# A hybrid decoder layer's mixture-of-experts step on one core: fixed expert order, three weight sets, and four smaller edits

## The chip, the core and the metric

The kernel runs on one NeuronCore of one Trainium2 chip. Its engines are TensorE (PE, matrix products into the PSUM banks), VectorE (DVE), ScalarE (ACT), GpSimd (POOL, which also issues the indirect transfers) and SyncE (SP, which issues nearly all others). The metric is the device time of one execution in microseconds, as the median of several runs.

## The reference

One layer over 1104 tokens: 64 tokens of 8 short sample sequences with states of their own, 16 meta tokens and 1024 prompt tokens. The mixer projects each token, applies a causal convolution, runs a gated delta rule (GDN, 4 heads) and a Mamba-2 recurrence (SSD, 8 heads), and projects back; the residual and a layer norm follow. Then comes a mixture of experts over the 1088 tokens that are kept (no meta tokens), two experts a token:

```python
def _moe(h, router_g, router_e, w1, w3, w2):
    g_val, g_idx = lax.top_k(g_prob, 1)
    ...
    e_val, e_idx = lax.top_k(jax.nn.softmax(e_logits, axis=-1), TOP_K)
    gate = g_val * e_val / jnp.sum(e_val, axis=-1, keepdims=True)
    expert = g_idx * E_PER_GROUP + e_idx
    ...
        xb = h[tok]
        return (jax.nn.silu(xb @ w1[e]) * (xb @ w3[e])) @ w2[e]
```

and y is the gate-weighted sum over a token's experts. D_MODEL is 1024, an expert is 512 wide, there are 32 experts. A last residual and layer norm give the output. Everything is float32.

## The kernel before, in words

The program is a chain of stages with a barrier between them. Each stage writes every engine's instructions by hand, so an engine's order is the order of its code, and semaphores (wait_ge, then_inc) join the engines.

**Projection and mixer.** After the projections, a mixer stage walks nine tiles: tile 0 holds the 64 sample tokens and the 16 meta tokens, tiles 1 to 8 hold 128 prompt tokens each. While tile 0 is worked, PE fills its waits with pieces of a gate projection (gate_part(n), L763). For tile 0 the state of every sample sequence has to be read: sample_ssd multiplies 32 state tiles (4 chunks ch[c] by 8 sequences, the state being the stationary operand) with 8 columns each (L974), ScalarE copies the result to rh, and 4 transposes (L979) turn it round. sample_gdn does the same with 16 columns (L1002), copies to rs, and adds rs with products against the identity (L1011, L1017). Both rs and rh hang on a memset (m_rs) for which PE waits at the start of the stage.

In the prompt loop, i is the tile in preparation, p = i-1 the one being finished, r = i-2 the one whose layer-normed row x1 goes through x1_transpose (L931), x1_copy (L1253) and router (L938). out_project (L962) is the projection back. In the last two rounds nothing is prepared, and PE does x1_transpose and router of tile 7 ahead of mix_transpose (L945, L948) and out_project of tile 8.

**Router stage.** DVE works out top-1 group, top-2 experts, the counts per expert, and a slot for each of the 2176 token-expert pairs in blocks of 96 (BLK). An expert has at least one block. Blocks lie in the order of the experts; table[0] is the last block's number and table[1 + n] block n's expert. SP loads expert 0's weights meanwhile (6 transfers of 1 MB: w13 in quarters q, w2 in halves).

**Expert stage.** A loop with a run-time end over the blocks. For block b PE does h_transpose(b-1) (L2116), x_transpose(b+1) (L2099), up(b) (L2109: 96 products, three thirds r, each ending in an e_up) and down(b-1) (L2130: 48 products in three thirds, each ending in an e_out). There is one set of w13 buffers and one of w2, so SP loads a quarter of the next block as soon as a third of up(b) has read its own (L2034), and w2 likewise after thirds of down (L2037); the very last block's w2 has buffers of its own (w2e). POOL gathers the block's 96 token rows into the one buffer xg (L2071) and adds the outputs to d_acc in HBM (L2077) from the one buffer eo. DVE's take(n) writes the row numbers to gather when block n-1 has been transposed, gate does the products with SiLU, and mark(n) the row numbers to add to, when the addition before has landed. ScalarE's evict(n) waits for both mark(n) and that addition.

**Final stage.** Nine tiles of d_acc are read back. DVE does the statistics of a tile (L2273, L2277, L2279), POOL the power -1/2 (L2315), DVE the shift (L2284), ScalarE the scaling (L2308), DVE the gain (L2289), POOL the offset (L2320) for seven tiles and DVE (L2292) for the last two; SP stores.

The input has 33 blocks: 33 additions to d_acc are in the trace, so one expert has two blocks and 31 have one.

## Time and profile before

| | |
|---|---|
| median of 3 runs | 1706.05 us (1699.59 to 1706.51) |
| the profiled execution: its own time, its span | 1698.48 us, 1696.6 us |
| busy share of the span: PE, DVE, ACT, POOL | 87%, 32%, 25%, 18% |
| mean granted TensorE clock | 0.938 of full |
| HBM read, written | 284.08 MB, 48.14 MB |
| mean DMA rate over the span | 193 GB/s |
| stages by their start in the trace | mixer 351 us, router 969 us, experts 1005 us, final 1650 us |

The times below are microseconds from the start of the span. The busy shares are means over stages that have different limits, so each stage has to be read by itself. The profiled execution lies at the fast end of the runs.

### The profile page before, as it was taken

How to read it: one execution, taken by the hardware profiler on the slowest of the kernel's cores; microseconds unless marked ns; L12 is line 12 of the kernel's file. 1: busy time of each engine (PE TensorE's matmuls, PEld its weight loads, DVE VectorE, ACT ScalarE, POOL GpSimd, SP SyncE). 2: the span in 40 equal slices, each digit the busy share in tenths (PEclk: the TensorE clock that was granted, in tenths of full speed). 3: DMA queues.
4: the chain of work that ended last, by engine and by line, in shares of the span. 5: the costliest groups of instructions: out<-in, count | busy, mean ns of one | idle time of the engine just before them, and what ended most of it. 6: DMA issues, size and time to landing. Idle time of an engine off the chain costs nothing. (4 is left out here: it accounts for less than half of the span.)

```text
span 1696.6 us, 34800 instructions
## 1 busy us (share of the span) xinstructions
PE 1477.5 (87%) x14148; PEld 977.6 (58%) x14148; DVE 545.9 (32%) x1257; ACT 427.8 (25%) x1207; POOL 297.2 (18%) x247
## 2 busy tenths in 40 slices
PE   8999999979898999999997528999999999899950
PEld 5666666657556777777775324555555555555530
DVE  2444444322134554445552251111111111111108
ACT  2211111131034344444342001222222222222212
POOL 0000000020114434224431000111111111111116
PEclk9999999998899999999999658999999999999985
DMA  7233332151325212222201246999999999999944
GB/s 255 78 91 80 78 79 69 51 173 40 113 77 209 87 44 75 100 100 82 97 29 38 91 184 221 375 379 383 376 366 378 377 373 378 383 369 373 384 114 190
DMA packets 119239, 328.24 MB, mean 193 GB/s; under 512 B 42712, under 2 KB 72328, under 8 KB 92552
## 3 DMA queue, kind: packets, MB, share of 16 engines
q1 hardware_dynamic: 110296, 300.59, 48.0%
q0 software_dynamic: 7728, 22.29, 5.6%
q10 hardware_dynamic: 1152, 4.52, 0.7%
q8 instruction: 39, 0.64, 0.2%
q14 instruction: 24, 0.20, 0.0%
HBM read 284.08 MB, written 48.14 MB: 196 GB/s over the span
## 5 line engine op out<-in xcount | busy, mean ns | idle before, releaser
L2109 PE MATMUL bank<-sb_arena 128*32 128x256 f32 x6336 | 352.2, 382 | 36.2 <-DMA sb_arena<-w 35.1
L387 PE MATMUL bank<-sb_arena 128*128 128x368 f32 x1056 | 329.8, 475 | 6.3 <-DMA sb_arena<-xT 6.3
L2109 PEld LDWEIGHTS bank<-sb_arena 128*32 128x32 f32 x6336 | 202.9, 111 | 175.8 <-DMA sb_arena<-w 40.8
L387 PEld LDWEIGHTS bank<-sb_arena 128*128 128x128 f32 x1056 | 201.3, 191 | 132.7 <-DMA sb_arena<-w_conv 6.3
L2130 PE MATMUL bank<-sb_arena 128*32 128x256 f32 x3168 | 177.8, 380 | 11.3 <-issue 6.7
L2130 PEld LDWEIGHTS bank<-sb_arena 128*32 128x32 f32 x3168 | 102.8, 110 | 83.8 <-issue 18.0
L962 PE MATMUL bank<-sb_arena 128*128 128x512 f32 (+1 forms) x288 | 133.9, 606 | 6.3 <-DVE sb_rlog L1566 5.0
L2216 DVE SCALAR_TENSOR_TENSOR sb_arena<-sb_arena,bank 128x128 f32<-128x128 f32 x99 | 28.6, 289 | 340.2 <-ACT sb_arena L2168 340.2
L2077 POOL DMA_INDIRECT d_acc<-sb_arena,sb_oidx x33 | 47.6, 1443 | 511.3 <-ACT sb_arena L2182 511.3
L2168 ACT ACTIVATE sb_arena<-bank 128x128 f32<-128x128 f32 x99 | 27.4, 277 | 373.8 <-PE bank L2109 373.8
L763 PE MATMUL bank<-sb_arena 128*128 128x384 f32 (+1 forms) x288 | 99.6, 499 | 8.5 <-DVE sb_arena L1582 8.5
L1516 DVE TENSOR_TENSOR sb_arena<-sb_arena,bank 128x256 f32<-128x256 f32 (+1 forms) x102 | 41.2, 412 | 153.8 <-PE bank L882 100.2
L962 PEld LDWEIGHTS bank<-sb_arena 128*128 128x128 f32 (+1 forms) x288 | 50.9, 188 | 60.6 <-issue 58.8
L763 PEld LDWEIGHTS bank<-sb_arena 128*128 128x128 f32 x288 | 55.9, 201 | 44.3 <-DVE sb_arena L1582 9.1
L459 DVE SCALAR_TENSOR_TENSOR sb_arena<-sb_arena 128x1040 f32<-128x1040 f32 x60 | 78.1, 1302 | 2.1
L1730 POOL TENSOR_TENSOR sb_arena<-sb_arena,sb_mask 128x512 f32<-128x512 f32 x48 | 72.6, 1519 | 13.2 <-DVE sb_arena L1425 4.9
L1763 POOL TENSOR_TENSOR sb_arena<-sb_arena 128x512 f32<-128x512 f32 (+1 forms) x9 | 11.0, 1220 | 363.8 <-ACT sb_arena L1158 363.8
L862 PE MATMUL bank<-sb_arena 128*128 128x128 f32 (+1 forms) x408 | 58.5, 290 | 14.8 <-DVE sb_arena L1516 14.2
L2208 DVE TENSOR_SCALAR sb_idx<-sb_slot 96x1 int32 (+1 forms) x35 | 5.2, 148 | 199.5 <-PE bank L2099 199.5
L862 PEld LDWEIGHTS bank<-sb_arena 128*128 128x128 f32 (+1 forms) x408 | 54.6, 202 | 25.5 <-issue 23.6
L1220 ACT ACTIVATE sb_arena<-bank 128x256 f32<-128x256 f32 (+1 forms) x102 | 38.6, 378 | 117.6 <-PE bank L862 114.8
L2181 ACT ACTIVATE sb_arena<-bank 96x256 f32<-96x256 f32 x99 | 37.5, 379 | 101.8 <-PE bank L2130 95.7
(325 smaller groups left out, 1710.8 us busy)
## 6 DMA issues: line engine op xcount, KB each, us to landing
sb_arena<-w SPq DMA_DIRECT2D x198, 1024.0 KB, 9.5
sb_arena<-w_conv SPq DMA_DIRECT2D x28, 512.0 KB, 4.8
sb_arena<-d_conv SPq DMA_DIRECT2D x7, 1792.0 KB, 7.1
d_conv<-sb_arena SPq DMA_DIRECT2D x22, 512.0 KB, 3.2
sb_arena<-d_gam SPq DMA_DIRECT2D x8, 768.0 KB, 3.9
d_x<-sb_arena SPq DMA_DIRECT2D x9, 512.0 KB, 2.7
sb_arena<-xT ACTq DMA_DIRECT2D x8, 552.0 KB, 9.2
sb_arena<-w_out SPq DMA_DIRECT2D x8, 512.0 KB, 7.1
```

Of the source, the lines that this page charges most:

```text
L387: last = e.matmul(bank[3 * r + s][:, 0:TN], wring[n % NV][:, k, :], xT[:, k, TN * s:TN * s + TN], start=(k == 0), stop=(k == KT - 1))
L459: e.scalar_tensor_tensor(aP, raw[r][:, i:i + TP], convw[:, n, i:i + 1], aP, ALU.mult, ALU.add)
L763: mm = e.matmul((D0, D1)[j % 2][:, 0:c1 - c0], gw[m % NSLOT][:, k, :], xT[:, k, c0:c1], start=(k == 0), stop=(k == KT - 1))
L862: last = e.matmul(bY[0:n, q * P:q * P + n], bt[level % 2][0:n, h0 + q, 0:n], X[0:n, h0 + q, 0:n], start=True, stop=True)
L962: last = e.matmul((D0, D1)[half][0:m, :], mixT[:, k, 0:m], wo[:, k, half * 512:(half + 1) * 512], start=(k == 0), stop=(k == KT - 1))
L1220: e.activation(ys[0:n, h0:h0 + 2, 0:n], heads(bY)[0:n, 0:2, 0:n], ACT.Copy).then_inc(S[f"lv_ys{s}"], 1)
L1516: e.tensor_tensor(d, d, heads(bZ)[0:n, 0:2, 0:n], ALU.subtract).then_inc(S[f"lv_x{s}"], 1)
L1730: e.tensor_tensor(bt[level % 2][0:n, :, 0:n], at[0:n, :, 0:n], bc1(mk(i)[0:n, LV + level, 0:n], n, GH, n), ALU.mult).then_inc(S["lv_bt"], 1)
L2077: e.indirect_dma_start(a["d_acc"], bass.IndirectOffsetOnAxis(ap=oidx[:, 0:1], axis=0), eo[0:BLK], None, compute_op=ALU.add).then_inc(S["e_ ...
L2109: mm = e.matmul(bank[r][j * CG:(j + 1) * CG, 0:2 * P], xgT[:, k, g * CG:(g + 1) * CG], w13[quarter_of(j, r)][:, k, :], start=(k == 0), sto ...
L2130: mm = e.matmul(bank[6 + r % 2][j * CG:(j + 1) * CG, 0:256], h, w[c // 2][:, k, (c % 2) * 256:(c % 2 + 1) * 256], start=(k == 0), stop=(k ...
L2181: e.activation(eo[0:BLK, r * 256:(r + 1) * 256], out[0:BLK, 0:256], ACT.Copy)
```

## The change

Five edits come together.

1. **Expert order and weights.** Blocks are worked in a new order: first the first block of each expert 0 to 31, then the blocks left over. order[n] is the place of the n-th worked block in the slot table; DVE reads it with a register load (place) ahead of take, gate and mark. There are three whole sets of weight buffers (NSET), with semaphores W of their own. Experts 0, 1 and 2 are loaded in the router stage, 18 transfers. In the expert stage SP's program is written out for experts 3 to 31, with fixed addresses, each quarter waiting for the third of up three blocks before; blocks left over are loaded into set 1 (LATER) alone, each after the block ahead of it. w2e is gone. PE's loop holds three blocks. The last block's outputs go to a buffer eo_last with row numbers oidx_last.
2. **Sample tokens of the mixer.** The 8 columns of each sequence are laid into zeroed tiles per_seq of 8 x 64 columns, which are now the stationary operand, and the states are the moving one, summed over the sequences in PSUM. rs, rh, their copies, the transposes and the products with the identity are gone.
3. **End of the prompt loop.** x1_transpose and router of tile 7 come after out_project of tile 8; DVE and ScalarE are reordered to match.
4. **Router stage.** The comparison that finds each block's expert has 22 columns in place of 54; five small instructions fill order.
5. **Final stage.** The gain and offset rows are copied into PSUM first and read from there in halves; the shift is another form of instruction; the statistics of tiles 1, 4 and 7 are done on ScalarE.

The core of the diff:

```diff
+                    gate_part(8)
+                    e.wait_ge(S["m_c"], 2)
...
-                            last = e.matmul(G1[:, c * TS + b * SL:c * TS + b * SL + SL], ch[c][:, b, :], cv[0][:, 18 + c // 2, b * SL:b * SL + SL], start=True, stop=True)
-                    last.then_inc(S["rh_ps"], 1)
-                    gate_part(8)
-                    e.wait_ge(S["rh"], 1)
-                    for c in range(4):
-                        last = e.transpose(G0[0:TS, c * P:(c + 1) * P], rh[:, c, :], ident[:])
+                            last = e.matmul(G0[0:TS, c * P:(c + 1) * P], per_seq[c // 2][:, b * TS:(b + 1) * TS], ch[c][:, b, :], start=(b == 0), stop=(b == SB - 1))
...
-                        e.wait_ge(S[f"ch_in{c}"], 32)
-                        for b in range(SB):
-                            last = e.matmul(G0.rearrange("p (h t s) -> p h t s", h=GH, t=2)[:, c, :, b * SL:b * SL + SL], ch[c][:, b, :],
-                                            qw[:, :, c, b * SL:b * SL + SL], start=True, stop=True)
-                    last.then_inc(S["rs_ps"], 1)
...
+                        e.wait_ge(S["m_w"], h + 1)
+                        e.wait_ge(S[f"ch_in{h}"], 32)
+                        e.matmul(G1[TS:T0, h * P:(h + 1) * P], XT[0:T0, h, TS:T0], vt[0][0:T0, h, :], start=True, stop=True)
+                        e.matmul(G1[0:TS, h * P:(h + 1) * P], XT[0:T0, h, 0:TS], vt[0][0:T0, h, :], start=True, stop=False)
+                        for b in range(SB):
+                            last = e.matmul(G1[0:TS, h * P:(h + 1) * P], per_seq[h % 2][:, b * TS:(b + 1) * TS], ch[h][:, b, :], start=False, stop=(b == SB - 1))
+                        if h < GH - 1:
+                            last.then_inc(S["w_ps"], 1)
+                            e.wait_ge(S["m_q"], h + 1)
+                        else:
+                            last.then_inc(S["u_ps"], 1)
+                            e.wait_ge(S["qd"], 1)
+                        for b in range(SB):
+                            last = e.matmul(G0[0:TS, h * P:(h + 1) * P], per_seq[2 + h % 2][:, b * TS:(b + 1) * TS], ch[h][:, b, :], start=(h == 0 and b == 0), stop=False)
+                        last.then_inc(S["r_ps"], 1)
...
-                        if tail:
-                            x1_transpose(r, 0)
-                            x1_transpose(r, 1)
-                            router(r)
                         if post:
                             e.wait_ge(S["st"], p + 1)
                             mix_transpose(p)
                             out_project(p, 0, 16)
+                        x1_transpose(r, 0)
+                        x1_transpose(r, 1)
+                        router(r)
                         continue
...
+                    if post and not prep:
+                        o_scale_a(p)
+                        s_update(p)
+                        o_scale_b(p)
+                        x1_gain(r)
+                        x1_add(r)
+                        mix_o(p)
+                        res_half(p, 0)
+                        continue
+                    if not prep:
+                        x1_gain(r)
+                        x1_add(r)
+                        logits(r - 1)
+                        logits(r)
+                        continue
...
-                    e.dma_start(w13[q].rearrange("p k n -> p (k n)"), a["w13"][0, q]).then_inc(S["r_w"], 16)
-                for h in range(2):
-                    e.dma_start(w2[h].rearrange("p k n -> p (k n)"), a["w2"][0, h]).then_inc(S["r_w"], 16)
+                for s in range(NSET):
+                    for q in (3, 0, 1, 2):
+                        e.dma_start(w13[s][q].rearrange("p k n -> p (k n)"), a["w13"][s, q]).then_inc(W["w13" + "abcd"[q] + str(s)], 16)
...
-                with e.Fori(1, last) as b:
-                    ex = expert(e.snap(b + 1))
-                    now = expert(b)
-                    e.wait_ge(S["e_up"], 3 * b + 1)
-                    load13(0, ex)
-                    e.wait_ge(S["e_up"], 3 * b + 2)
...
+                def first_down(ex):
+                    for h in range(2):
+                        e.wait_ge(S["e_out"], 3 * (ex - NSET + 1) + h)
+                        load2(h, ex % NSET, a["w2"][ex, h])
+
+                for ex in range(NSET, E):
+                    for q in (0, 1, 3, 2):
+                        e.wait_ge(S["e_up"], 3 * (ex - NSET) + min(q, 2) + 1)
+                        load13(q, ex % NSET, a["w13"][ex, q])
+                    if ex > NSET:
+                        first_down(ex - 1)
+                first_down(E - 1)
+                with e.Fori(E, last + 1) as b:
+                    ex = e.value_load(table[0:1, bass.ds(b - (E - 1), 1)], min_val=0, max_val=E - 1)
+                    e.wait_ge(S["e_up"], 3 * b - 2)
+                    load13(0, LATER, a["w13"][bass.ds(ex, 1), 0].rearrange("x p m -> p (x m)"))
...
                     e.wait_ge(S["e_out"], 3 * b)
-                    load2(w2, 0, now, "w2a")
+                    load2(0, LATER, a["w2"][bass.ds(ex, 1), 0].rearrange("x p m -> p (x m)"))
                     e.wait_ge(S["e_out"], 3 * b + 1)
-                    load2(w2, 1, now, "w2b")
+                    load2(1, LATER, a["w2"][bass.ds(ex, 1), 1].rearrange("x p m -> p (x m)"))
...
-                    scatter(n)
+                    e.wait_ge(S["e_go"], 1)
+                    e.wait_ge(S["e_eo"], n)
+                    e.indirect_dma_start(a["d_acc"], bass.IndirectOffsetOnAxis(ap=oidx_last[:, 0:1], axis=0), eo_last[0:BLK], None, compute_op=ALU.add).then_inc(S["e_st"], 16)
...
+                def up(n, s, load):
+                    e.wait_ge(W[f"w13d{s}"], 16 * load)
                     for r in range(NR):
-                        e.wait_ge(S["w13" + "abc"[r]], 16 * n + 16)
+                        e.wait_ge(W["w13" + "abc"[r] + str(s)], 16 * load)
...
-                with e.Fori(1, last + 1) as b:
+                with e.Fori(0, (E - 2) // NSET) as i:
+                    for j in range(NSET):
+                        before, s = e.snap(NSET * i + j), (j + 1) % NSET
+                        h_transpose(before)
+                        x_transpose(e.snap(NSET * i + (j + 2)))
+                        up(e.snap(NSET * i + (j + 1)), s, e.snap(i + (2 if s == 0 else 1) + (AHEAD if s == LATER else 0)))
+                        down(before, j, e.snap(i + 1 + (AHEAD if j == LATER else 0)))
+                h_transpose(E - 2)
+                x_transpose(E)
+                up(E - 1, LATER, E - 1)
+                down(E - 2, 0, (E - 2) // NSET + 1)
...
-                    down(before, w2)
+                    up(b, LATER, b)
+                    down(before, LATER, before)
                 h_transpose(last)
-                e.wait_ge(S["w2e"], 32)
-                down(last, w2e)
+                down(last, LATER, last)
...
+                e.wait_ge(S["e_og"], last + 1)
+                for r in range(NR):
+                    e.wait_ge(S["e_out"], 3 * last + (r + 2))
...
+                    e.activation(eo_last[0:BLK, r * 256:(r + 1) * 256], out[0:BLK, 0:256], ACT.Copy)
+                    if r == 2:
+                        e.wait_ge(S["e_st"], 16 * last + 16)
...
+                def place(n):
+                    return e.value_load(order[0:1, bass.ds(n, 1)], min_val=0, max_val=NBMAX)
+
                 def take(n, first=False):
+                    at = place(n)
...
                 def mark(n):
+                    at = place(n)
                     e.wait_ge(S["e_st"], 16 * n + 16)
-                    e.tensor_scalar(oidx[:], slot[0:BLK, bass.ds(n, 1)], 1.0, None, ALU.mult).then_inc(S["e_og"], 1)
+                    e.tensor_scalar(oidx[:], slot[0:BLK, bass.ds(at, 1)], 1.0, None, ALU.mult).then_inc(S["e_og"], 1)
...
-                    e.scalar_tensor_tensor(rv[t][0:n, 2:3], mv2[t][0:n, 0:1], -1.0, rv[t][0:n, 1:2], ALU.mult, ALU.mult).then_inc(S["c_nmr"], 1)
+                    if t in BY_ACT:
...
+                        step = e.tensor_scalar(rv[t][0:n, 2:3], mv2[t][0:n, 0:1], rv[t][0:n, 1:2], -1.0, ALU.mult, ALU.mult)
...
-                    e.tensor_tensor(rows[t][0:n], rows[t][0:n], lnrow[0:n, 0, :], ALU.mult).then_inc(S["c_g"], 1)
+                    for s in range(2):
+                        half = rows[t][0:n, s * 512:(s + 1) * 512]
+                        last = e.tensor_tensor(half, half, bank[s][0:n, :], ALU.mult)
...
-                        e.tensor_tensor(rows[t][0:n], rows[t][0:n], lnrow[0:n, 1, :], ALU.add).then_inc(S["c_yv"], 1)
-
-                e.memset(rv[0][0:1, 3:4], 0.0).then_inc(S["c_go"], 1)
+                        for s in range(2):
+                            half = rows[t][0:n, s * 512:(s + 1) * 512]
+                            last = e.tensor_tensor(half, half, bank[2 + s][0:n, :], ALU.add)
+                        last.then_inc(S["c_yv"], 1)
...
+                for q in range(4):
+                    last = e.tensor_copy(bank[q][:], lnrow[:, q // 2, (q % 2) * 512:(q % 2 + 1) * 512])
+                last.then_inc(S["c_ln"], 1)
+                e.wait_ge(S["c_ln"], 1)
...
+                    if t < NTT and t not in BY_ACT:
                         stats(t)
...
-                for t in range(NTT):
...
+                    e.activation(junk[t][0][0:n], rows[t][0:n], ACT.Copy, accum_out=st[t][0:n, 0, 0:1]).then_inc(S["c_sum"], 1)
...
+                    e.activation(junk[t][1][0:n], rows[t][0:n], ACT.Square, bias=st[t][0:n, 0, 1:2], accum_out=st[t][0:n, 0, 2:3]).then_inc(S["c_sq"], 1)
```

The order in which PE's instructions stand, ahead of the loop's end in the expert stage, before. The rows are the body of the loop, one block: h_transpose, x_transpose, up, down, and the branch back.

```order
L2116 MATMUL bank<-sb_ident,sb_arena 128x128 x3
L2095 ISA
L2099 MATMUL bank<-sb_ident,sb_arena 128x96 x8
L2103 ISA
L2109 MATMUL bank<-sb_arena 32x256 x96
L2123 REGISTER_ALU
L2130 MATMUL bank<-sb_arena 32x256 x48
L2137 ISA
L2137 COMPARE_AND_BRANCH
```

The same engine and place in the changed kernel. Two blocks that read like this one stand ahead of it in the same body.

```order
L2170 ISA
L2173 MATMUL bank<-sb_ident,sb_arena 128x128 x3
L2152 ISA
L2156 MATMUL bank<-sb_ident,sb_arena 128x96 x8
L2160 ISA
L2166 MATMUL bank<-sb_arena 32x256 x96
L2182 REGISTER_ALU
L2189 MATMUL bank<-sb_arena 32x256 x48
L2196 REGISTER_ALU
L2196 COMPARE_AND_BRANCH
```

The body has grown from one block to three, and the branch back comes once for three blocks.

The order of PE's instructions in sample_gdn, before: L763 is a piece of the gate projection, L1002 the states against 16 columns, L1010 and L1011 the first head's product and its addition by the identity.

```order
L763 MATMUL bank<-sb_arena 128x384 x8
L1002 MATMUL bank<-sb_arena 128x2x8 x32
L763 MATMUL bank<-sb_arena 128x336 x8
L1010 MATMUL bank<-sb_arena 80x128
L1011 MATMUL bank<-sb_ident,sb_arena 80x128
```

The same place in the changed kernel. L777 is the gate projection; L1022 and L1030 are one head's states as moving operand, 8 sequences each.

```order
L777 MATMUL bank<-sb_arena 128x384 x8
L777 MATMUL bank<-sb_arena 128x336 x8
L1019 MATMUL bank<-sb_arena 16x128
L1020 MATMUL bank<-sb_arena 64x128
L1022 MATMUL bank<-sb_arena 64x128 x8
L1030 MATMUL bank<-sb_arena 64x128 x8
```

The 32 products ahead of the piece of the gate projection have become 16 for each of four heads behind it, and the identity products are gone.

The order of PE's instructions at the end of the prompt loop, before: L853 ends the last state product, L931 and L938 are x1_transpose and router, L945 and L948 mix_transpose, L962 out_project.

```order
L853 MATMUL bank<-sb_arena 128x128 x4
L931 MATMUL bank<-sb_ident,sb_arena 128x128 x8
L938 MATMUL bank<-sb_arena 128x36 x8
L945 MATMUL bank<-sb_ident,sb_arena 128x128 x4
L948 MATMUL bank<-sb_ident,sb_arena 128x128 x4
L962 MATMUL bank<-sb_arena 128x512 x16
L931 MATMUL bank<-sb_ident,sb_arena 128x128 x8
L938 MATMUL bank<-sb_arena 128x36 x8
```

The same place in the changed kernel: L949 and L956 are x1_transpose and router, L963 and L966 mix_transpose, L980 out_project.

```order
L867 MATMUL bank<-sb_arena 128x128 x4
L963 MATMUL bank<-sb_ident,sb_arena 128x128 x4
L966 MATMUL bank<-sb_ident,sb_arena 128x128 x4
L980 MATMUL bank<-sb_arena 128x512 x16
L949 MATMUL bank<-sb_ident,sb_arena 128x128 x8
L956 MATMUL bank<-sb_arena 128x36 x8
L949 MATMUL bank<-sb_ident,sb_arena 128x128 x8
L956 MATMUL bank<-sb_arena 128x36 x8
```

x1_transpose and router of tile 7 have moved from ahead of mix_transpose and out_project of tile 8 to behind them.

## Rows read from the trace of the kernel before

**Rows 1.** Busy time by stretch: length; busy us (instructions) of PE, PEld, DVE, ACT, POOL; clock; DMA share; GB/s.

```profile
969.00:987.00 18.00, 2.29 (x4) 1.17 (x4) 13.53 (x52) 0.44 (x2) 0.00 (x0) 0.50 0.97 395
...
1041.00:1613.00 572.00, 529.66 (x9277) 319.00 (x9277) 70.19 (x281) 135.03 (x372) 73.57 (x61) 1.00 1.01 372
```

**Rows 2.** Waits of PE, 1010 to 1640: total us, times, longest.

```profile
PE bank L2109 <- DMA sb_arena<-w: 35.1, 29, 2.3
```

**Rows 3.** Timeline, 1590 to 1697: start, us, instruction [idle before <- releaser].

```profile
1595.71 10.57 PE L2109 MATMUL bank<-sb_arena 128*32 128x256 f32 x192 [1.11 <-DMA sb_arena<-w]
...
1612.70 10.57 PE L2109 MATMUL bank<-sb_arena 128*32 128x256 f32 x192
...
1636.74 1.93 PE L2130 MATMUL bank<-sb_arena 128*32 128x256 f32 x32 [3.15 <-ACT sb_arena L2182]
```

**Rows 4.** DMA, 1020 to 1600: packets, MB, share; issues, KB, us to landing.

```profile
q0 software_dynamic: 6808, 20.08, 14.5%
q8 instruction: 3, 0.05, 0.0%
...
sb_arena<-w SPq DMA_DIRECT2D x185, 1024.0 KB, 9.5
sb_arena<-d_x,sb_idx POOLq DMA_INDIRECT x32, 10.8
```

**Rows 5.** Timeline, 1000 to 1697: the start of the expert stage.

```profile
1004.71 0.91 DVE L2224 MEMSET sb_arena<- 128x1024 f32 x1 [2.89 <-issue]
...
1007.72 1.18 POOL L2071 DMA_INDIRECT sb_arena<-d_x,sb_idx  x1 [50.00 <-DVE sb_arena L2226]
...
1015.13 1.54 PE L2099 MATMUL bank<-sb_ident,sb_arena 96*128 96x96 f32 x8 [15.35 <-DMA sb_arena<-d_x,sb_idx]
...
1040.85 12.48 PE L2109 MATMUL bank<-sb_arena 128*32 128x256 f32 x192
```

**Rows 6.** Timeline of PE, 378 to 446 (first three) and 440 to 540: sample tokens.

```profile
395.91 10.23 PE L974 MATMUL bank<-sb_arena 128*128 128x8 f32 x64
...
405.99 7.35 PE L763 MATMUL bank<-sb_arena 128*128 128x384 f32 x16
...
414.77 5.43 PE L763 MATMUL bank<-sb_arena 128*128 128x384 f32 x16
...
445.96 3.64 PE L1002 MATMUL bank<-sb_arena 128*128 128x16 f32 x32
...
461.23 6.39 PE L763 MATMUL bank<-sb_arena 128*128 128x336 f32 x16
...
476.38 1.15 PE L1022 MATMUL bank<-sb_arena 16*128 16x128 f32 x8
```

**Rows 7.** Waits of PE, 380 to 470.

```profile
PE bank L1002 <- DMA sb_arena<-state_gdn: 4.6, 2, 2.9
```

**Rows 8.** Timeline, 913 to 1006: the last two tiles of the mixer.

```profile
926.59 1.11 PE L931 MATMUL bank<-sb_ident,sb_arena 128*128 128x128 f32 x4 [5.18 <-DVE sb_arena L1385]
...
933.63 1.09 PE L945 MATMUL bank<-sb_ident,sb_arena 128*128 128x128 f32 x4
...
936.85 16.72 PE L962 MATMUL bank<-sb_arena 128*128 128x512 f32 x32 [1.28 <-DVE sb_arena L1561]
...
953.61 0.69 DVE L1357 SCALAR_TENSOR_TENSOR sb_arena<-sb_arena,bank 128x512 f32<-128x512 f32 x1 [6.07 <-PE bank L962]
...
959.17 0.72 PEld L931 LDWEIGHTS bank<-sb_ident,sb_arena 128*128 128x128 f32 x4 [6.43 <-DVE sb_arena L1385]
```

**Rows 9.** Groups of instructions, 1653 to 1697: busy us, mean ns, idle before.

```profile
L2273 DVE BATCH_NORM_STATS2 sb_arena<-sb_arena 128x6 f32<-128x512 f32 (+1 forms) x18 | 11.5, 676 | 3.5 <-DMA sb_arena<-d_acc 3.5
...
L2315 POOL TENSOR_TENSOR sb_arena<-sb_arena,sb_mhalf 128x1 f32<-128x1 f32 (+1 forms) x9 | 11.0, 1228 | 20.3 <-DVE sb_arena L2279 20.3
```

**Rows 10.** Timeline, 1590 to 1697 and 870 to 1000: single instructions of POOL and DVE.

```profile
1657.13 0.56 POOL L2315 TENSOR_TENSOR sb_arena<-sb_arena,sb_mhalf 128x1 f32<-128x1 f32 x1 [1.11 <-DVE sb_arena L2279]
...
870.50 0.69 DVE L1482 TENSOR_TENSOR sb_arena<-bank,sb_arena 128x512 f32<-128x512 f32 x1 [1.31 <-PE bank L838]
```

245 lines of the change are left out of this document (147 added, 98 removed).

## The prediction

> **What bounds the kernel now.** I read the table of stretches first. In the expert stage, 1041 to 1613, PE is busy 530 of 572 us at the full clock, and the 16 DMA engines are busy throughout at 372 GB/s [rows 1]. So two limits lie close together there, and the other views have to say which one ends last. PE's waits name it: before its first products of a block, PE waits for a weight transfer 29 times, 35.1 us in all [rows 2]. The timeline shows both cases. The up products of one block start at 1595.71 after 1.11 us of such a wait, those of the next at 1612.70 with none, so a block takes PE 16.99 us when its weights are there [rows 3]. From 1040.85 [rows 5] to 1612.70 there are 31 blocks in 571.9 us, 18.45 us each. That is the pace of the transfers: a block's weights are 6.29 MB, its gather and its addition another 20.08 MB / 31 = 0.65 MB [rows 4], and 6.94 MB in 18.45 us is 376 GB/s. The stage is bound by its transfers, with PE 1.46 us a block behind. The router stage is the opposite: in its first 18 us the DMA engines move expert 0's weights at 395 GB/s [rows 1], and then they rest until the expert stage.
>
> **The expert stage, -30 us.** The bytes are the same, 33 x 6.29 MB; 12.6 MB of them move into the time of the router stage. At 395 GB/s that alone is worth 32 us, if no engine becomes the limit before.
> Start: three sets are 18.9 MB, 48 us from 969, landed by 1017; PE's first transposes start at 1015.13 [rows 5]. The first gather, issued at 1007.72, fed them 7.4 us later with the DMA engines free. Now they are loaded, and a gather under load lands after 10.8 us [rows 4], so 3.4 us later. DVE's register load of the place stands ahead of it. The trace has no such load on DVE, but one, of table[0], lies within the 2.89 us of idle ahead of 1004.71 [rows 5], so it costs between 0 and 2.9 us; I take 0, since most of that idle time must be the barrier. In the loop it is hidden: in take and gate DVE waits for PE anyway; in mark it delays oidx, behind which ScalarE's evict and POOL's addition are queued, and PE would wait for evict in the last third of down. Up(1) then starts at about 1044 instead of 1040.85.
> PE's own limit: 30 blocks more at 17.0 us, up(31) at 1554.
> The transfers' limit: the first buffers come free with the first third of up(1), about 1047.5. From there SP is never held up, since PE frees a set every 17.0 us and the DMA engines need 18.45 for one. Expert 4's four quarters take 12.3 us (4/6 of 18.45), each later expert 18.45: those of expert 31 are there at 1047.5 + 12.3 + 27 x 18.45 = 1558, 4 us later than PE wants them. PE begins on three of the four quarters, so up(31) starts at about 1557. The two limits meet at the end of the fixed part: the lead from the router stage is used up just there.
> Last block: the left-over block has one set for itself, set 1, which up(31) is still reading. Its first quarter can be asked for a third, 3.5 us, into up(31), the last two at its end, and ahead of them in SP's queue stand w2 of experts 30 and 31, 12.3 us from 1558 to 1570. Three quarters more take 8.4 us and some 2 us to land: up(32) at 1581, where PE would have been ready at 1574. It ends at 1591.5, and down(31), half as many products, at 1597. w2 of the left-over block is asked for only when down(31) has read the old one, and lands at about 1602; PE wants it at 1599. The last products end at 1608. Before, they end at 1636.74 + 1.93 = 1638.7, and that includes the wait of 3.15 us [rows 3] for the addition ahead of it, which eo_last takes away. Difference -30.
> Bounds: were transfers no limit at all, up(32) would start at 1571 and all end at 1597, -41. Were the rate 365 GB/s (3% less), the same steps give 1626, -12.
>
> **The sample tokens, -8 us.** Before, 64 passes with 8 columns (32 products, two passes each) take 10.1 us, and the gate piece behind them 7.35 us [rows 6]; the next piece of its kind, at 414.77, takes 5.4, so the clock had fallen in between. Now 64 passes with 128 columns and a stationary tile of 64; the gate piece comes first. The nearest row for a pass is L1002 at 445.96, 32 passes in 3.64 us, 0.114 us each [rows 6], so 7.3 us. With 4 transposes gone that is 10.1 + 7.35 + 0.5 against 5.4 + 7.3: -5. In sample_gdn, from 445.96 to 476.38, 30.4 us, 4.6 us are waits for states that are still being loaded [rows 7], and after each of them PE is slower for a time (the gate piece at 461.23 takes 6.39). Now: gate piece 5.4, four heads of 36 passes at 0.114, 16.4; gate piece 5.4; four products 0.9: 28.1, -2, and the third head's state is wanted 8 us later in the sequence than before, so that wait goes. At the start of the stage PE no longer waits for a memset, less than 1. Sum -8. Bounds: a pass may cost 0.157 us as in L974, whose 64 take 10.1: 192 passes more by 0.043, +8, so 0; or the state waits and slow clock go altogether, -11. New waits stand in the heads: on ScalarE's w_columns and on POOL's q_columns, for heads 2 and 3 each behind the head two before; each is one copy of 64 columns and has a head's 4 us to hide in.
>
> **The end of the prompt loop, -6 us.** x1_transpose and router of tile 7 hold PE from 926.59 to 933.63, and out_project of tile 8 starts at 936.85, 3.2 us after mix_transpose begins [rows 8]. With them out of the way mix_transpose waits for the scaling of tile 8's output only. DVE does o_scale before s_update now, so it can start about 925 to 926.5: out_project 7 to 9 us earlier. Behind out_project the 7.0 us of PE's work stand beside the 5.6 us in which DVE works out tile 8's rows (953.61 to 959.17), and tile 8's transposes wait for them (rlog): 1.5 us back. -6, between -4 and -7.5.
>
> **The router stage, 0.** DVE's two comparisons shrink and five small instructions come in, ahead of a wait for PE; PE's work starts no sooner. -1 to +1. SP issues 18 transfers for 6 beside DVE's work, and no longer waits for weights at the end.
>
> **The final stage, -7 us.** POOL's power takes 0.56 us at 1657.13 [rows 10], but 1.23 on average over its nine [rows 9]: an instruction of one column that takes a microsecond is held up. What runs beside the slow ones and not beside the first is DVE's gain, a product of two operands in SBUF. A DVE product with one operand in PSUM takes 0.69 us for half a row at 870.50, beside POOL's work [rows 10]. With the gain read from PSUM nine powers take 5.0 us in place of 11.0, -6, and POOL's power and offset follow each other without a gap before, so all of it shortens the stage; DVE, held up in turn by POOL's offsets, gives 1 to 4 more. The gain itself grows to two instructions of 0.69, and ScalarE's statistics of a tile, which read it twice, delay the scaling of the tile ahead: 1 to 2 back. The four copies into PSUM, 4 x 0.69 = 2.8 us, stand in the 3.5 us in which DVE waits for the first tile [rows 9]; without that cover they would cost all of it. -7. Bounds: POOL stays held up, 0; all holding up goes, -11.
> The Trainium skill (SBUF — State Buffer, Who interferes with whom) has it that VectorE and GpSimd share a pair of ports as an exclusive lock, which a VectorE instruction with two SBUF inputs takes against a GpSimd one that reads SBUF. By that rule all of the holding up goes, the -11 end; the trace agrees as far as 0.56 against 1.23 us shows.
>
> **Sum.** -30 -8 -6 +0 -7 = -51 against the profiled execution's own 1698.5 us: 1647.5. The median of the runs lies 7.6 above that execution and the lowest 1.1; I predict 1649.
>
> **Rivals.**
> PE's code is fetched again at each branch back. In 580 us of the loop PE's instruction queue (q8) moves 3 packets, 0.05 MB [rows 4], so the body of one block stays where it is. The new body is three times as long. If it does not fit, each of 9 branches stops PE for one transfer. No row has the price: a weight transfer lands after 9.5 us under load [rows 4], a free gather after 7.4, and next to nothing is the other end. I take 4: 9 stops make 36 us, of which 11 stand in waits for weights that PE has in the forecast. 25 more: 1674.
> The Trainium skill (Runtime: NRT & Kernel Launch, Instruction fetch mechanics) gives PE a buffer of 128 KiB and says that a branch to code outside the window stops the engine for a fetch. Three blocks are 3 x 598 instructions of 64 bytes, 112 KiB, an estimate from that page that leaves 16 KiB to spare at best, and the page speaks of a smaller window too.
> The same, dearer, is the way to slower: 9 x 7 - 11 = 52, so from 7 us a branch on the whole gain is gone, and at 9.5 us the time is 1647.5 + 74.5 = 1722.
> The transfers run below 372 GB/s with more of them queued: at 365, 18 more, 1665.
> The early loads buy nothing in the expert stage, because gathers behind deeper queues set the pace. A gather has to land inside a block's 17.0 us; it takes 10.8 now. If it takes some 15, the pace is 18.45 again and only the other edits' 21 us are left: 1680. Against it: the loads queued now already keep the engines busy throughout.
>
> **Numbers.** Forecast 0.60, own range 1632 to 1662. Refetching at a middling price 0.17 (1674). Lower rate 0.12 (1665). Gathers 0.06 (1680). Refetching at full price 0.05 (1722). The range 1631 to 1676 takes in the forecast's range, the lower rate and the cheaper half of refetching, 0.8. 0.5% is about what a measurement of this kernel can tell from none, 8.5 us: faster than 1697.5 0.91, within 0.5% 0.05, slower 0.04.
>
> **What would show it.** Right: gaps between the starts of up of 17.0 us, with few waits on weights before block 25; a wait of about 7 us ahead of up(32) and of some 3 ahead of the last down; 395 GB/s from 969 to 1017; the power at 0.56 us in all tiles; out_project of tile 8 within 10 us of the last state product. Wrong: instruction packets by the dozen in the loop with PE idle every third block; gathers landing after 14 us; passes of 0.15 us in the sample products; a stage still at 18.45 a block.

## The result, and the profile after

Slower. The median is 1744.7 us (1740.5 to 1748.3) against 1703.5 for the kernel before beside it, ratio 1.024 (95% interval 1.021 to 1.028). The prediction was 1649 with 1631 to 1676, so it is outside on the slow side, and even beyond what I gave as refetching at full price (1722). The profiled execution has a span of 1746.5 us, 49.9 longer than before.

The page of the changed kernel already has the pattern. Busy tenths of PE in 40 slices of the span, granted clock, DMA, and the instruction queue:

```profile
PE 1497.3 (86%) x14200; PEld 981.6 (56%) x14200; DVE 539.5 (31%) x1269; ACT 435.4 (25%) x1227; POOL 290.8 (17%) x250
...
PE   8999999899989999999986287977977987897970
...
PEclk9999999999989999999997588988988988998985
DMA  7233323152351222211103979989989988988545
...
q8 instruction: 138, 2.26, 0.6%
```

In the right third of the rows, from the start of the expert stage on, most slices have a PEclk of 8 and a dip in PE; a round of three blocks is 1.45 slices long. q8, the instruction queue, has 138 packets. The row on the page of the kernel before has 39, and 3 of them fall in 580 us of its loop [rows 4]:

```profile
q8 instruction: 39, 0.64, 0.2%
```

PE's waits from 950 to 1700 (total us, times, longest), to be read beside [rows 2]:

```profile
PE bank L2173 <- issue: 54.2, 9, 6.6
PE bank L2156 <- issue: 33.7, 9, 4.0
...
PE bank L2189 <- DMA sb_arena<-w: 6.6, 1, 6.6
```

The 29 waits for weights ahead of up are gone; one of 6.6 us is left, ahead of the last products. In their place PE stands idle twice for each of nine branches back, and "issue" says that no data and no semaphore released it. The timeline of PE around one of them:

```profile
1088.79 12.66 PE L2166 MATMUL bank<-sb_arena 128*32 128x256 f32 x192
...
1107.70 10.57 PE L2166 MATMUL bank<-sb_arena 128*32 128x256 f32 x192
...
1124.52 10.57 PE L2166 MATMUL bank<-sb_arena 128*32 128x256 f32 x192
1134.90 5.36 PE L2189 MATMUL bank<-sb_arena 128*32 128x256 f32 x96
1146.22 0.90 PE L2173 MATMUL bank<-sb_ident,sb_arena 128*128 128x128 f32 x3 [5.95 <-issue]
1146.91 1.17 PE L2156 MATMUL bank<-sb_ident,sb_arena 96*128 96x96 f32 x6
1151.93 0.48 PE L2156 MATMUL bank<-sb_ident,sb_arena 96*128 96x96 f32 x2 [3.86 <-issue]
1152.34 13.30 PE L2166 MATMUL bank<-sb_arena 128*32 128x256 f32 x192
```

Between the branches the starts of up are 16.82 us apart, as wanted (1107.70, 1124.52). At the branch PE is idle for 5.95 us at the head of the loop and 3.86 more in the middle of x_transpose, and the up behind it takes 13.30 us in place of 10.57. One round of three blocks takes 1146.22 - 1082.67 = 63.55 us, where 3 x 16.82 are 50.5: 13.1 us a branch, 118 for nine. The clock's share of that, by stretches (length; busy us of PE, PEld, DVE, ACT, POOL; clock; DMA share; GB/s):

```profile
1088.80:1101.40 12.60, 12.60 (x197) 6.66 (x200) 1.59 (x6) 0.56 (x2) 0.98 (x1) 0.83 0.55 175
1107.70:1118.10 10.40, 10.40 (x195) 6.28 (x198) 1.59 (x6) 0.85 (x3) 2.42 (x2) 1.00 1.01 356
1082.70:1146.20 63.50, 53.71 (x897) 31.75 (x897) 7.14 (x27) 13.07 (x36) 7.25 (x6) 0.90 0.92 333
1041.00:1613.00 572.00, 484.09 (x8077) 286.58 (x8073) 64.25 (x243) 117.63 (x324) 65.37 (x54) 0.90 0.92 331
```

In the up behind a stop the granted clock is 0.83 of full on average, in the next one 1.00; against [rows 1] the stage's DMA rate has fallen from 372 to 331 GB/s, because PE frees no buffers while it is idle.

The rest of the program did about what was forecast. The sample tokens, PE's timeline beside [rows 6]:

```profile
391.40 9.89 PE L777 MATMUL bank<-sb_arena 128*128 128x336 f32 x32
401.21 7.20 PE L994 MATMUL bank<-sb_arena 128*64 128x128 f32 x64
...
445.67 1.91 PE L1022 MATMUL bank<-sb_arena 128*64 128x128 f32 x16
447.41 1.91 PE L1030 MATMUL bank<-sb_arena 128*64 128x128 f32 x16
...
468.17 1.15 PE L1040 MATMUL bank<-sb_arena 16*128 16x128 f32 x8
```

The end of the prompt loop, beside [rows 8]:

```profile
914.02 1.06 PE L867 MATMUL bank<-sb_arena 128*128 128x128 f32 x8
...
921.00 16.36 PE L980 MATMUL bank<-sb_arena 128*128 128x512 f32 x32 [1.28 <-DVE sb_arena L1585]
```

The final stage by lines, beside [rows 9] (count | busy us, mean ns | idle before):

```profile
L2437 POOL TENSOR_TENSOR sb_arena<-sb_arena,sb_mhalf 128x1 f32<-128x1 f32 (+1 forms) x9 | 4.9, 548 | 19.9 <-DVE sb_arena L2368 16.9 <-ACT sb_arena L2416 3.0
```

### The profile page after: what moved, and what is told of

The parts are those of the page before. It is cut to its first block and busy times, and to the rows that moved or that the text cites. A ratio compares the mean times of both kernels' runs of the same rounds, so it can differ in the third digit from the quotient of the medians.

```text
span 1746.5 us, 34532 instructions
## 1 busy us (share of the span) xinstructions
PE 1497.3 (86%) x14200; PEld 981.6 (56%) x14200; DVE 539.5 (31%) x1269; ACT 435.4 (25%) x1227; POOL 290.8 (17%) x250
## 5 line engine op out<-in xcount | busy, mean ns | idle before, releaser
L2166 PE MATMUL bank<-sb_arena 128*32 128x256 f32 x6336 | 371.3, 397 | 1.0 <-ACT sb_arena L2227 1.0
L2189 PE MATMUL bank<-sb_arena 128*32 128x256 f32 x3168 | 179.1, 382 | 6.6 <-DMA sb_arena<-w 6.6
L980 PE MATMUL bank<-sb_arena 128*128 128x512 f32 (+1 forms) x288 | 133.6, 604 | 6.3 <-DVE sb_rlog L1590 5.0
L777 PE MATMUL bank<-sb_arena 128*128 128x384 f32 (+1 forms) x288 | 96.1, 486 | 7.7 <-PEq L150 7.7
L2290 DVE TENSOR_SCALAR sb_idx<-sb_slot 96x1 int32 x35 | 5.2, 148 | 266.9 <-PE bank L2156 266.4
L2156 PE MATMUL bank<-sb_ident,sb_arena 96*128 96x96 f32 x272 | 36.9, 284 | 57.5 <-issue 33.7
L980 PEld LDWEIGHTS bank<-sb_arena 128*128 128x128 f32 (+1 forms) x288 | 50.7, 188 | 60.4 <-issue 58.5
L777 PEld LDWEIGHTS bank<-sb_arena 128*128 128x128 f32 x288 | 54.3, 194 | 42.6 <-issue 13.2
L876 PE MATMUL bank<-sb_arena 128*128 128x128 f32 (+1 forms) x408 | 57.9, 288 | 14.8 <-DVE sb_arena L1540 14.1
L2173 PE MATMUL bank<-sb_ident,sb_arena 128*128 128x128 f32 x99 | 21.2, 331 | 54.6 <-issue 54.2
L1244 ACT ACTIVATE sb_arena<-bank 128x256 f32<-128x256 f32 (+1 forms) x102 | 38.6, 378 | 117.0 <-PE bank L876 114.1
```

Of the source, the lines that this page charges most:

```text
L777: mm = e.matmul((D0, D1)[j % 2][:, 0:c1 - c0], gw[m % NSLOT][:, k, :], xT[:, k, c0:c1], start=(k == 0), stop=(k == KT - 1))
L876: last = e.matmul(bY[0:n, q * P:q * P + n], bt[level % 2][0:n, h0 + q, 0:n], X[0:n, h0 + q, 0:n], start=True, stop=True)
L980: last = e.matmul((D0, D1)[half][0:m, :], mixT[:, k, 0:m], wo[:, k, half * 512:(half + 1) * 512], start=(k == 0), stop=(k == KT - 1))
L1244: e.activation(ys[0:n, h0:h0 + 2, 0:n], heads(bY)[0:n, 0:2, 0:n], ACT.Copy).then_inc(S[f"lv_ys{s}"], 1)
L2156: mm = e.transpose(bank[3 + k // 4][:, (k % 4) * BLK:(k % 4 + 1) * BLK], xg[0:BLK, k * P:(k + 1) * P], ident[0:BLK, 0:BLK])
L2166: mm = e.matmul(bank[r][j * CG:(j + 1) * CG, 0:2 * P], xgT[:, k, g * CG:(g + 1) * CG], w13[s][quarter_of(j, r)][:, k, :], start=(k == 0), ...
```

## The experiments

The question was which of three things made PE stop: code fetched again because the loop's body had grown (the rival of the prediction), something in the new order or the three weight sets (gathers, DVE's register loads), or the loaded DMA engines behind either. After that: why the expert stage, with the stops gone, gives so little.

**1. No branch back.** PE's 30 blocks written out one behind the other.

```diff
-                with e.Fori(0, (E - 2) // NSET) as i:
-                    for j in range(NSET):
...
+                for before in range(E - 2):
+                    h_transpose(before)
+                    x_transpose(before + 2)
+                    for n, part in ((before + 1, up), (before, down)):
+                        part(n, n % NSET, n // NSET + 1 + (AHEAD if n % NSET == LATER else 0))
```

> The changed kernel, but PE's 30 blocks of the fixed part are written out one behind the other in place of ten rounds of a loop of three; no other engine changes. If the time went to PE's code being fetched again at each branch back (9 branches, each two stops of 6.1 and 3.8 us and some 3 us of slower products behind them, 13.1 us together), all of it comes back and the transfers' limit comes in near the end: 1645 us (1635 to 1660), no stop at every third block, starts of up 16.8 us apart. If the loss lies in something else that the three sets, the gathers or the registers on DVE bring, PE's order being the same, the time stays at 1735 or more. If code in a straight line cannot be fetched fast enough beside loaded DMA engines either (38 KB a block), there are shorter stops spread over all blocks and 1670 to 1720.

Measured: 1666.4 us, 0.979 of before (0.978 to 0.980). All stops are gone, and 78 us with them. Only PE's branches back, and the register arithmetic that goes with a loop, were taken out; the order, the three sets, DVE's register loads and the full DMA engines stayed. So none of these stops PE by itself, and the branches back are what does; how much longer the full DMA engines make a stop is left to run 7, and the register arithmetic to runs 2 to 4. But it isn't 1645, and it is outside the range that was expected (1635 to 1660). PE's waits, 940 to 1700:

```profile
PE bank L2166 <- DMA sb_arena<-w: 23.5, 14, 4.8
PE bank L2189 <- DMA sb_arena<-w: 13.4, 7, 7.5
```

37 us of waits for weights are there, against 6.6 with the stops: of the 118 us that the nine branches cost in PE's own time, 30 come back as these waits, which is most of what lies between 118 and 78. Its q8 moves 113 packets, 66 more than a kernel with two blocks in a loop (run 6) for 28 more blocks: 2.36 packets of 16.4 KB, 38.6 KB, a block. Three blocks are 116 KB. The queue's rows on the pages of this run and of run 6:

```profile
q8 instruction: 113, 1.85, 0.5%
```

```profile
q8 instruction: 47, 0.77, 0.2%
```

**2. Six blocks in the loop**, 4 branches back.

```diff
-                with e.Fori(0, (E - 2) // NSET) as i:
-                    for j in range(NSET):
-                        before, s = e.snap(NSET * i + j), (j + 1) % NSET
+                with e.Fori(0, (E - 2) // 6) as i:
+                    for j in range(6):
+                        before, s = e.snap(6 * i + j), (j + 1) % NSET
...
```

> The changed kernel, but PE's loop holds six blocks in place of three: 4 branches back in place of 9. If a branch back costs the same whatever the size of the body, 5 x 13.1 us fewer: 1682 us (1670 to 1692). If the price grows with the body (the whole body fetched before PE goes on), 4 x 26 us stay of 9 x 13: 1733.

Measured: 1680.2 us (0.987; 0.985 to 0.988). Two stops at each of four branches:

```profile
PE bank L2173 <- issue: 23.1, 4, 5.9
PE bank L2156 <- issue: 14.3, 4, 3.7
```

That is 5.8 + 3.6 us a branch, nearly the 6.0 + 3.7 of the changed kernel, with a body twice as long: PE waits for the head of the loop, not for the whole body. The whole body is moved all the same. The page has 124 packets on q8; a kernel without a loop has 113, of which 24 blocks too many for this one are some 57, so four branches moved some 68, 17 each, for a body of 14.

**3 and 4. The kernel before, with two and with three blocks in PE's loop** for the first 30 blocks, and nothing else changed, so that size stands alone. The diff is that of the run with two; the other has ten rounds of three.

```diff
-                with e.Fori(1, last + 1) as b:
-                    before = e.snap(b - 1)
+                with e.Fori(0, 15) as i:
+                    for j in range(2):
+                        before, b = e.snap(2 * i + j), e.snap(2 * i + (j + 1))
...
+                with e.Fori(31, last + 1) as b:
```

> The kernel before, but PE's loop holds two blocks for the first 30 (15 rounds, 14 branches back), and nothing else changes. One block's code is about 38 KB, two are 77 KB. If 77 KB stay in place: 1700 us, no difference. If two blocks are already fetched again, 14 branches at 10 to 13 us: 1840 to 1880.

> The kernel before, but PE's loop holds three blocks for the first 30 (10 rounds, 9 branches back), and nothing else changes: one set of weights, the order of before. If refetching is a matter of the body's length alone, 9 branches at 10 to 13 us: 1790 to 1815 us, with two stops at each. If it was the changed kernel's own sets or order that stopped PE: 1700, no difference.

Measured: two blocks 1703.8 us (1.001; 1.000 to 1.002), three blocks 1753.5 (1.030; 1.028 to 1.033). Two blocks, 77 KB, stay where they are; three, 116 KB, are fetched again. Both loops have register arithmetic of the same kind, so that is not what stops PE. The queue's row on the two pages:

```profile
q8 instruction: 44, 0.72, 0.2%
```

```profile
q8 instruction: 127, 2.08, 0.5%
```

83 packets more; two of them and a half are the one block more of code, so some 9 packets a branch, where the body has 7. In the changed kernel a round of 63.5 us moves 10. I read this as fetching that runs on past the body's end and is thrown away with each branch; one packet of it may be that a body does not begin and end with a piece. Three blocks cost less here (+51 us, where 90 to 115 were expected). Each branch has one stop, not two, and 12 of the 35 us of waits for weights are gone (22.7 left), as the transfers gain on PE while it is idle:

```profile
PE bank L2116 <- issue: 46.6, 9, 6.0
```

**5. Where the second stop comes from.** In the changed kernel it falls some 20 instructions behind the head of the loop. 64 tiny transposes, two instructions each, were put where PE waits 16.6 us for its first gather, so that they move the loop's code (that they also keep PE busy there is what the second run is for); then 128 of them as the control. By the size of the body some 256 instructions are one packet of the queue: a block has 598 (299 passes and as many weight loads) and 2.36 packets.

```diff
+                for _ in range(64):
+                    e.transpose(bank[5][0:8, 0:32], ident[0:32, 0:8], ident[0:32, 0:32])
                 x_transpose(0, first=True)
```

> The changed kernel, with 64 tiny transposes (128 instructions of PE) put ahead of its first transposes of the expert stage, where PE waits 16.6 us for a gather; they only move the loop's code by half of a 16 KB fetch. In the changed kernel there are two stops at each branch, one at the loop's head, one 20 instructions later. If the second comes because the head stands just ahead of the end of a fetched piece, it is gone or has moved behind a longer run: one stop of about 6 us a branch, 9 x 3.8 = 34 us fewer waits, 1705 to 1715. If it comes from the deeper queue of weight transfers beside it, both stops stay where they are: 1745.

> As the kernel with 64 tiny transposes, but with 128 of them (256 instructions), so that the loop's code is moved by one whole 16 KB fetch. If the place of the loop's head within such a fetch makes the second stop, both stops are back where they were: 9 x (6 + 3.8) us in PE's waits, and 1740 to 1745 us. If the padding worked by something else (a warmer clock at the start), one stop of 5 us a branch, as with 64, and 1700.

Measured, one execution each: 1700.9 us with 64, 1741.9 with 128. With 64:

```profile
PE bank L2173 <- issue: 46.0, 9, 5.4
```

With 128:

```profile
PE bank L2173 <- issue: 54.0, 9, 6.8
PE bank L2156 <- issue: 32.8, 9, 3.9
```

So the second stop is a matter of place: it goes when the code is moved by half a packet and is back when it is moved by a whole one. My reading, which no run shows directly, is that when the head stands just ahead of the end of a fetched piece, the first piece holds only a few instructions and PE runs dry before the second is there. Each of the two is a single execution, but the 41 us between them are in their own stops too (46.0 against 54.0 + 32.8). So much of the changed kernel's time hung on where its loop happened to begin.

**6. Two weight sets, two blocks in the loop** (NSET = 2, one line).

> The changed kernel with two weight sets in place of three, and so a loop of two blocks on PE (15 rounds). Two blocks' code stayed in place in the kernel before, so no stop is expected, and no code is fetched in the loop. The lead is one expert (6.3 MB, 16.8 us at 375 GB/s) shorter than in the straight kernel: 1666 + 17 = 1683 us (1675 to 1690), transfer waits from about block 8 on. If code is fetched again here all the same, 14 branches at 13 us: over 1800. If the lead is worth nothing, 1666.

Measured: 1665.8 us (0.979; 0.978 to 0.981), no stop, q8 at 47 packets, and as fast as three sets written out. The 17 us that a third set was expected to bring do not show. PE's timeline at the start shows one half of why. Two sets:

```profile
994.84 13.25 PE L2166 MATMUL bank<-sb_arena 128*32 128x256 f32 x192 [0.96 <-ACT sb_arena L2227]
```

Three sets, written out:

```profile
1001.25 12.98 PE L2166 MATMUL bank<-sb_arena 128*32 128x256 f32 x192 [0.96 <-ACT sb_arena L2225]
```

PE's first up starts 6.4 us earlier. Of these, 4.3 are a shorter wait for the first gather, which has six transfers fewer ahead of it (12.2 us against 16.5); the other 2.1 this execution already had when it issued the gather (987.73 against 989.80), 1.7 of them at the start of the router stage, ahead of anything that differs between the two kernels. The other half is the rate, in the part of each in which the transfers are the limit. Two sets, blocks 12 to 30:

```profile
1205.53:1539.97 334.44, 308.63 (x5383) 185.96 (x5383) 42.88 (x163) 78.41 (x216) 43.64 (x37) 0.99 1.02 381
```

Three sets, blocks 18 to 31:

```profile
1315.25:1560.50 245.25, 224.09 (x3887) 138.26 (x3888) 30.60 (x115) 56.36 (x156) 29.11 (x25) 0.99 1.01 374
```

18 blocks in 334.4 us are 18.58 each; 13 in 245.2 are 18.87. With two blocks in the loop there is no q8 traffic; written out, q8 holds 0.8 to 0.9% of the DMA engines' time for 0.5% of the bytes. That this traffic is what makes the 0.3 us a block was not tried by itself.

**7. The stops with the DMA engines nearly free.** The changed kernel, each weight transfer of the expert stage cut to 256 of 2048 columns.

```diff
-                    e.dma_start(w13[s][q].rearrange("p k n -> p (k n)"), src)...
+                    e.dma_start(w13[s][q].rearrange("p k n -> p (k n)")[:, 0:256], src[:, 0:256])...
```

> The changed kernel, but each weight transfer of the expert stage brings only the first 256 of 2048 columns (from expert 3 on; the products then use what is left of older weights in the rest). PE's code and order are those of the changed kernel. If the stops are the code fetch's own latency, they stay: 6.1 and 3.8 us, nine times each, and only the wait before the last block goes: 1730 to 1738. If the code stands behind weight transfers in the DMA engines, the stops shrink to half or less: 1680 to 1705.

Measured, one execution: 1696.7 us. PE's waits:

```profile
PE bank L2173 <- issue: 30.9, 9, 3.7
PE bank L2156 <- issue: 22.6, 9, 3.1
```

The time lies in the second range (1680 to 1705), but the stops did not shrink to half: of 88 us, 53 stay at a DMA rate of 78 GB/s in place of 332 (1100 to 1500). So 3.8 us a branch hang on the traffic around the fetch and 5.9 do not go with it; as some traffic is left, those 5.9 are an upper bound for the fetch alone. Of the 48 us that this run gains on the changed kernel 34 are in the stops; most of the rest are shorter waits for weights and gathers (6.4) and a router stage that starts 3.5 us earlier.

**8. The other edits alone**, with the router and expert stages of before.

> The kernel before with the sample-token edit, the end of the prompt loop and the final stage of the changed kernel, but with the router and expert stages of before. By the changed kernel's own trace these edits brought the start of the router stage 15.8 us earlier and took 7.7 us out of the final stage: 1698.5 - 15.8 - 7.7 = 1675 (1670 to 1682). If part of those gains is only taken up by a wait for transfers in the expert stage, 1685 or more.

Measured: 1673.9 us (0.984; 0.983 to 0.985). As expected. The new router and expert stages are therefore worth only 1666.4 - 1673.9 = -7.5 us even without the stops (by the two ratios, each against the kernel before beside it, -8.7).

**9 to 11. More out of it.** All give the last block's w2 buffers of its own again, asked for at the start of the expert stage: with three sets written out; with two sets; with three sets of which the third is asked for at the start of the expert stage too.

```diff
+                end = e.value_load(table[0:1, bass.ds(last - (E - 1), 1)], min_val=0, max_val=E - 1)
+                for h in range(2):
+                    e.dma_start(w2e[h].rearrange("p k n -> p (k n)"), a["w2"][bass.ds(end, 1), h]...).then_inc(S["w2e"], 16)
...
-                down(last, LATER, last)
+                down(last, LATER, last, w2e)
```

> The straight kernel (30 blocks written out), and the last block's w2 has two buffers of its own again, asked for at the start of the expert stage, when the DMA engines are half idle. In the straight kernel PE waits 7.5 us for that transfer and then works 2.9 us slower: if that wait is all there is, 1666 - 10 = 1656 us (1652 to 1660). If the transfers are simply short of time, the 2.1 MB earlier only shift the same wait to the blocks before: 1664 to 1668.

> Two weight sets and a loop of two blocks, and the last block's w2 in buffers of its own, asked for at the start of the expert stage. There the DMA engines are at 116 to 225 GB/s until 1020 in the kernel with two sets, so the 2.1 MB cost nothing, and the wait of 6.8 us before the last products goes with the 1.8 us of slower work behind it: 1665.8 - 8 = 1658 (1654 to 1662). If that transfer only pushes the first gathers back and the transfers stay the limit, 1663 to 1667.

> The straight kernel with the early w2, and the third set's six transfers asked for at the start of the expert stage and not in the router stage, so that the first gather has less ahead of it. In the kernel with two sets PE's first up starts at 994.8, in the straight one at 1001.3, after 16.5 us of waiting for the gather: if that delay was the price of the third set, 1664.4 - 5 = 1659 (1656 to 1662). If code fetches and deeper queues make the transfers 1 to 2% slower and that is the limit, 1664, and two sets stay the better choice.

Measured: 1664.4 us (0.977; 0.975 to 0.979), 1661.3 (0.977; 0.975 to 0.979), 1662.1 (0.977; 0.975 to 0.979). The wait before the last products goes in all three, and 2 to 5 us come of it, not 8 to 10; the intervals overlap those of runs 1 and 6, so the last few us between these five kernels are not told apart. Run 11 does not settle what the third set costs at the start, because its edit does not take the transfers out of the gather's way: SP issues them at 984.5 and POOL the first gather only at 987.9, and that gather feeds PE 9.2 us after its issue, against 9.0 in run 1 and 4.6 with two sets. The first up starts at 999.6, not at 995, and the wait for the second gather is longer (9.6 us against 8.5 in run 9). About 1661 to 1666 is what this design gives, 2.1 to 2.3% below the kernel before.

## Why the prediction was wrong

**The step that failed** is the choice between forecast and rival: that the loop's three blocks stay in place (0.60 for the forecast, 0.22 for refetching in both of its forms). The runs showed the opposite: the three blocks, 116 KB, are fetched again at each of nine branches back. Removing the branches gives 78 us back; that alone turns the sign of the result. The rival named the mechanism and the rows that would show it, and both came: instruction packets by the dozen, PE idle every third block. The Trainium skill (Runtime: NRT & Kernel Launch, Instruction fetch mechanics) gives PE a buffer of 128 KiB, and by it I had 16 KiB to spare. What is measured is less: 77 KB stay and 116 KB do not. The smaller window that the prediction read there does not bear on these loops either, since two blocks stay with 6 packets in 580 us. Since 9 to 10 packets are moved for a body of 7, I take it that part of the room goes to what is fetched ahead of PE (no run shows the room). A body that by that page fills seven eighths of a buffer need not stay in it; that belonged into the chance.

**The price** was missing from the rows, and I put it at 4 us, the middle between nothing and a transfer's landing. It is 13.1 us a branch in the changed kernel: 6.0 at the head, 3.7 at the end of the first piece, 3.3 by the lower clock behind them. The bound that I took from [rows 4], 9.5 us for one transfer under load, was no bound, because a branch can cost two fetches and the clock comes on top. In the kernel before with three blocks, with one stop, it is 5.2 us of stop, and 5.7 us of time after what the waits for weights give back.

**The expert stage, -30.** Without the stops it is -7.5, the router stage included (runs 1 and 8). From the first up to up(31) the written-out kernel takes 1560.50 - 1001.25 = 559.3 us, before 578.1; I had forecast 536. Three terms of the sum were mis-sized. The transfers' pace beside PE's is 18.87 us a block, not 18.45, over 27.7 blocks 11.6 us. I left w2 of expert 3 out of what has to come after the first free buffer (2.1 MB, 5.6 us): SP can ask for it only after down(0), behind expert 4's quarters. And the DMA engines are not full from 1028 on, when the first third of up(1) is read, but from 1042: 84 GB/s from 1020 to 1030 and 324 to 1042, which is some 3 us of transfers (290 GB/s over 1028 to 1042 against 375 later). Together they are 20 of the 23 us. PE's own pace is 16.82, not 17.0, so it uses up its lead faster: waits return with block 17, not near 31. At the end, from up(31) to the last product, it takes 55.7 us (51 forecast, 43 before). What was right is the direction of each: the bytes move to the router stage (413 GB/s from 953 to 971, 386 in the changed kernel itself), and then the engines rest as before while the first gathers land, which is where the lead goes.

**The first gather under load**, +3.4 us forecast: from the start of the router stage to the first transposes 47.6 us against 46.5, +1.0. The gather feeds PE 9.0 us after its issue in place of 7.4, +1.6, half of the forecast, and the router stage gives 0.6 back. With two sets it takes 4.6, less than before.

**The sample tokens, -8.** The next chunk starts at 499.29 and not at 507.50: -8.2. Passes take 0.112 us as in the row chosen, the states are waited for nowhere, the heads take 4.18 us each. Of the 8.2, 6.3 are left at the end of the prompt loop (907.54 against 913.87).

**The end of the prompt loop, -6.** out_project of tile 8 starts 5.9 us after the last state product and 15.9 us earlier than before; the router stage starts 15.8 us earlier, 9.5 more than the 6.3 already there. More than the -7.5 of my bound, on two counts: out_project itself moves by 9.5 us where I had 7 to 9, and I gave 1.5 us back for tile 8's transposes, which do wait (1.36 us), but x1_transpose and router of tile 7 take 4.6 us behind out_project, at the full clock (937.21 to 941.82), in place of the 7.0 that I moved.

**The router stage, 0.** From its start to the first memset of the expert stage 35.5 us against 36.1.

**The final stage, -7.** From the last product to the end 49.6 us against 57.9, -8.3. The power takes 0.55 us in all nine tiles (1.23 on average before [rows 9]). The Trainium skill's rule on the shared ports (SBUF — State Buffer, Who interferes with whom) has this trace on its side: with the gain's second operand in PSUM no power is held up. From 1724.38 on POOL's powers and offsets follow each other without a gap. No run changes that operand alone; the shift and the statistics changed with it.

**Sum.** Start of the router stage -15.8, up to the first transposes +1.0, expert stage +73.0 (696.5 us against 623.5), final stage -8.3: +49.9, the difference of the spans.

**What stays open.** How large a body may be between 77 and 116 KB, what of the lead a third set would keep if its transfers were asked for behind the first gather, and by how much the deeper queue slows the weights apart from the code's traffic (18.58 a block with two sets, 18.50 before, 18.87 written out with both at once).

## What to carry to other kernels

Growing the body of a hardware loop has a cliff that no instruction count of the engines shows: measure the code of a body in the instruction queue's packets, and leave room for what is fetched ahead (here two blocks of 38.6 KB cost nothing, three cost 6 to 13 us at every branch back). If buffers that rotate force a body of several blocks, take the smaller ring (two sets, two blocks in the loop), or write the loop out; both gave 1666 us here, where the ring of three in a loop gave 1745. And before a deeper ring is built, look where its head start would be spent: here the limit was bytes, the engines rested again at the stage's start, and the third set brought nothing that could be measured.

## What the runs showed that was not expected

- A branch back to code that is gone costs one or two fetches depending on where the loop's head lies: moved by 128 instructions the kernel took 1700.9 us, by 256 it took 1741.9 (one execution each), unmoved 1744.7.
- Of the 9.8 us of stops a branch, 3.8 depend on the load of the DMA engines; the rest is still there at a quarter of the rate (78 GB/s against 332).
- Code written out streams beside 375 GB/s of weights without stopping PE once in 30 blocks, 38.6 KB a block, at 0.8 to 0.9% of the DMA engines' time.
